# Gate and up of a feed-forward by Strassen's seven block products, in a kernel of two transformer blocks

## The chip, the cores and the metric

The kernel runs on one core of one Trainium2 chip. The metric is the device time of one execution in microseconds (us), the median of the runs shown.

## The reference, cut to what matters

Two blocks are computed one after the other on 512 tokens of 1024 channels (and 256 context tokens in the first), in float32. Among attention, a recurrent mixer and the modulation vectors they hold five feed-forwards; three of them (the latent tokens' in layer 1, and two in the second block) are what the change touches:

```python
def swiglu(h, w_in, w_out):              # h: 512 x 1024, hidden width 2816
    g, u = jnp.split(h @ w_in, 2, axis=-1)
    return (jax.nn.silu(g) * u) @ w_out
```

## The kernel before, in words

**Numbers.** Every product is made in three: both factors are split into a high part (rounded by ACT's copy to fp32r) and a low part (the rest), and high x high, low x high and high x low are added in PSUM (`product`, line 342). A weight block is [128, 8, 128] and comes by DMA into one of four `raw` slots (`load_block`, L308), ACT writes `w_hi` (`split_hi`, L317), POOL writes `w_lo` (`split_lo`, L323). The semaphores `hi_ready`, `lo_ready` and `w_used` count blocks over the whole program.

**A feed-forward** has 22 chunks of 128 hidden channels: a gate block, an up block and an out block for each. Group 0 to 9 (`ffn_groups`, line 1015, the `step` functions) takes four gate and up blocks (chunks 2g+1 and 2g+2) and two out blocks (chunks 2g and 2g+1); a last group, cut into token halves, follows. In a gate or up block PE does 8 x 3 products of 512 tokens (`in_block`, line 1029); for the out blocks 8 output tiles n, each 2 x 3 products, alternately in the PSUM banks 5 and 6. ACT takes the silu of the gate (L1197), DVE multiplies it with up (L1292), ACT and DVE split the hidden chunk (L1204, L1297), and DVE adds each output tile to `y` (L1357), which frees its bank. For l1_ffn and s_ffn1 DVE's queue also holds four modulation ops per group (`mods`, L406, and the copy of L460), 1024 columns each, fed by their own loads. s_ffn2 has none.

**What sets the order.** Each engine's queue is in program order, written out by hand in `ffn_pe`, `ffn_act`, `ffn_dve`, POOL's stage of `split_lo` and SP's stream of loads. The inner groups of the three feed-forwards are a hardware loop of two groups a turn; those of l0_ffn and l0_ffnc are unrolled. The feed-forwards l0_ffn and l0_ffnc are not touched.

## Time and profile before

| | |
|---|---|
| median of 3 runs | 2802.25 us (2801.66 to 2803.56) |
| profiled execution, span | 2801.8 us |
| PE busy | 2725.5 us (97%) |
| DVE, ACT, POOL busy | 1607.7, 1078.9, 1241.0 us |
| loaded weight blocks | 441 of 512 KB |

The profiled execution is one of its own, with 2801.8 us from its first to its last instruction; it is within the runs' spread. PE is TensorE, DVE VectorE, ACT ScalarE, POOL GpSimd, SP SyncE, which issues the loads. Busy PE time is modelled, since matmuls overlap; what one costs in a row of them is the distance between their starts. The granted clock is 1.00 at 2.4 GHz and 0.50 at 1.2 GHz.

### The profile page before, as it was taken

Reading aid. Unit: us, or ns where it says so; the run is one execution under the profiler, and the core shown is the slowest. Engines: PE = TensorE matmul, PEld = TensorE weight load, DVE = VectorE, ACT = ScalarE, POOL = GpSimd, SP = SyncE. Lnnn points to the kernel's source line nnn. Section 1 sums busy time; section 2 is a strip of 40 time slices with the busy share of each in tenths; the row PEclk is TensorE's granted clock in tenths of the full one; section 3 lists DMA queues with packets and bytes.
Section 4 is the critical chain, followed back from the end, with each engine's and each line's share of the span. In section 5 each row is a group of like instructions: output and inputs, shape, how many; then the busy total and the mean of one; then the engine's idle time right before and its main releaser. Section 6 shows DMA issues by size and latency. Waiting matters only on the chain.

```text
span 2801.8 us, 41300 instructions
## 1 busy us (share of the span) xinstructions
PE 2725.5 (97%) x15728; PEld 2353.3 (84%) x15728; DVE 1607.7 (57%) x2597; ACT 1078.9 (39%) x1817; POOL 1241.0 (44%) x646
## 2 busy tenths in 40 slices
PE   8989999999999999999999999999989999999998
PEld 6778888788999899988888888888877788888887
DVE  6788766677776678456556655555563512422223
ACT  3267332233445367442222332222464833422222
POOL 0333554445566433345544355444433344444443
PEclk8999999999999999999999999999999999999999
DMA  5323555443576422234544245442323233132221
GB/s 238 107 49 95 203 211 188 143 143 120 202 254 213 144 54 62 76 121 159 174 162 155 71 160 173 162 157 98 124 50 113 76 105 98 62 102 93 96 90 60
DMA packets 103865, 361.70 MB, mean 129 GB/s; under 512 B 12449, under 2 KB 14625, under 8 KB 102305
## 3 DMA queue, kind: packets, MB, share of 16 engines
q1 hardware_dynamic: 103714, 359.63, 38.6%
q8 instruction: 102, 1.67, 0.2%
q14 instruction: 49, 0.40, 0.0%
HBM read 338.61 MB, written 2.10 MB: 122 GB/s over the span
## 4 chain that ended last, share of the span: by engine, by line
PE 86%; DVE 8%; ACT 2%; issue 1%; POOL 1%; DMA 1%; POOLq 0%; SPq 0%; ACTq 0%; DVEq 0%
PE ps L346 73%; PE ps L2273 3%; PE ps L2261 2%; PE ps L2243 2%; PE ps L753 1%; DVE negm L2322 1%; PE ps L423 1%; PE ps L2466 1%; PE ps L573 1%; PE ps L2246 1%; PE ps L2028 1%; DVE dump L406 1%; POOL w_lo L323 1%; ACT prob L2295 0%; ACT w_hi L317 0%
## 5 line engine op out<-in xcount | busy, mean ns | idle before, releaser
L323 POOL TENSOR_TENSOR w_lo<-raw,w_hi 128x1024 fp32r<-128x1024 f32 x421 | 1076.4, 2565 | 1187.6 <-ACT w_hi L317 1156.2
L317 ACT ACTIVATE w_hi<-raw 128x1024 fp32r<-128x1024 f32 x441 | 460.4, 1056 | 1143.2 <-PE ps L346 1104.3
L346 PE MATMUL ps<-n_hi,w_hi 128*128 128x512 f32 (+1 forms) x1744 | 639.0, 366 | 10.5 <-DVE n_lo L880 9.5
L346 PE MATMUL ps<-n_lo,w_hi 128*128 128x512 f32 (+1 forms) x1744 | 627.2, 360 | 0.0
L346 PE MATMUL ps<-n_hi,w_lo 128*128 128x512 f32 (+1 forms) x1744 | 627.2, 360 | 0.0
L346 PEld LDWEIGHTS ps<-n_hi,w_hi 128*128 128x128 f32 x1744 | 328.6, 188 | 66.9 <-DVE n_lo L880 9.8
L346 PEld LDWEIGHTS ps<-n_lo,w_hi 128*128 128x128 f32 x1744 | 328.9, 189 | 51.0 <-issue 1.9
L346 PE MATMUL ps<-h_hi,w_hi 128*128 128x512 f32 (+1 forms) x1096 | 363.1, 346 | 8.8 <-DVE h_lo L622 4.4
L346 PEld LDWEIGHTS ps<-n_hi,w_lo 128*128 128x128 f32 x1744 | 328.6, 188 | 49.4
L346 PE MATMUL ps<-h_lo,w_hi 128*128 128x512 f32 (+1 forms) x1096 | 356.6, 340 | 0.0
L346 PE MATMUL ps<-h_hi,w_lo 128*128 128x512 f32 (+1 forms) x1096 | 356.5, 340 | 0.0
L346 PE MATMUL ps<-ffn_hi,w_hi 128*128 128x512 f32 (+1 forms) x928 | 334.0, 360 | 5.1 <-DVE y L1357 2.2
L346 PE MATMUL ps<-ffn_lo,w_hi 128*128 128x512 f32 (+1 forms) x928 | 332.9, 359 | 0.0
L346 PE MATMUL ps<-ffn_hi,w_lo 128*128 128x512 f32 (+1 forms) x928 | 332.6, 358 | 0.0
L1357 DVE TENSOR_TENSOR y<-y,ps 128x512 f32<-128x512 f32 x288 | 197.7, 687 | 188.5 <-PE ps L346 188.5
L1292 DVE TENSOR_TENSOR ps<-ffn_silu,ps 128x512 f32<-128x512 f32 (+1 forms) x107 | 68.3, 639 | 294.3 <-PE ps L346 272.1
L346 PEld LDWEIGHTS ps<-h_hi,w_hi 128*128 128x128 f32 x1096 | 201.6, 190 | 35.8 <-issue 10.3
L346 PEld LDWEIGHTS ps<-h_lo,w_hi 128*128 128x128 f32 x1096 | 201.1, 190 | 25.7 <-issue 2.2
L346 PEld LDWEIGHTS ps<-h_hi,w_lo 128*128 128x128 f32 x1096 | 200.8, 190 | 23.3
L346 PEld LDWEIGHTS ps<-ffn_hi,w_hi 128*128 128x128 f32 x928 | 175.6, 189 | 32.0 <-DVE y L1357 2.6
L406 DVE CUSTOM_DVE_ANT_0 dump<-mod_extra,modraw 128x1024 f32<-128x1024 f32 x93 | 197.8, 2127 | 4.3
L346 PEld LDWEIGHTS ps<-ffn_hi,w_lo 128*128 128x128 f32 x928 | 175.7, 189 | 25.8
(329 smaller groups left out, 3868.0 us busy)
## 6 DMA issues: line engine op xcount, KB each, us to landing
raw<-w_stream SPq DMA_DIRECT2D x441, 512.0 KB, 3.5
modraw<-mod_stream SPq DMA_DIRECT2D x88, 512.0 KB, 4.9
mod_extra<-mod_stream SPq DMA_DIRECT2D x88, 512.0 KB, 5.3
mod_pair<-mod_first SPq DMA_DIRECT2D x7, 1024.0 KB, 12.5
l_qs<-l_q_hi SPq DMA_DIRECT2D x32, 128.0 KB, 2.3
l_qs<-l_q_lo SPq DMA_DIRECT2D x32, 128.0 KB, 2.3
l_qs<-l_q_hi SPq DMA_DIRECT2D x16, 192.0 KB, 2.9
l_qs<-l_q_lo SPq DMA_DIRECT2D x16, 192.0 KB, 3.5
```

The source lines that it names most:

```text
L317: nc.scalar.activation(w_hi[:, c % RING, :], raw[:, c % RING, :], ACT.Copy).then_inc(hi_ready, 1)
L323: nc.gpsimd.tensor_tensor(w_lo[:, c % RING, :], raw[:, c % RING, :], w_hi[:, c % RING, :].bitcast(F32), ALU.subtract).then_inc(lo_ready, 1)
L346: mm = nc.tensor.matmul(out, w[a], x[b][:, off:off + n], start=first and i == 0, stop=last and i == 2)
L406: nc.vector.tensor_tensor_reduce(where, mod_slot(p), row, 1.0, 0.0, ALU.mult, ALU.add, outs[j]).then_inc(mod_ops, 1)
L423: mm = nc.tensor.matmul(ps[:, 3, 2 * k:2 * k + 2], mod_pairs[k][:, 0, j * P:(j + 1) * P], c_cols[:, j, :], start=j == 0, stop=j == KC - 1)
L573: mm = nc.tensor.matmul(ps[:, SUM_BANK[name] + i, 0:n], ones[:, :], buf, start=k == 0, stop=k == KC - 1)
L753: mm = nc.tensor.matmul(half(bank)[:, t * P + i:t * P + i + SUM_COLS], squares_[:, slot, t * P:(t + 1) * P], ones[:, 0:SUM_COLS], start=Tr ...
L1292: nc.vector.tensor_tensor(up_bank(f, m % 2), f["silu"][:, m % 2, 0:f["n"]], up_bank(f, m % 2), ALU.mult).then_inc(sem(f["tag"] + "_hid"), 1)
L1357: ins = nc.vector.tensor_tensor(acc, acc, out_bank(f, 8 * g + n), ALU.add)
L2243: mm = nc.tensor.matmul(score(a, i, col, w), a["qs"][head % 2][:, j, x[2]:x[2] + P], k[:, kc, kcol:kcol + w], start=j == 0, stop=j == 1 an ...
L2261: mm = nc.tensor.transpose(ps[:, 4 + g, (b - b0) * P:(b - b0 + 1) * P], prob[:, i % 2, b * P:(b + 1) * P], ident)
L2273: mm = nc.tensor.matmul(head_out(i), a["v"][z][:, blocks[b], a["vcol"](c, x)], a["pt"][p][:, i % 2, b * P:(b + 1) * P], start=b == 0 and j ...
```

## The change

In groups 1 to 9 of the three feed-forwards gate and up of a chunk are one product of a 2 x 2 block matrix (rows gate and up, columns the two halves of the 1024 channels) with a 2 x 2 block matrix of the input (channel halves by token halves), by the Winograd form of Strassen's scheme. With A11, A12 the gate's halves and A21, A22 the up's, the weight sides of the seven products are A11, A12, A22, S1 = A21 + A22, S2 = S1 - A11, S3 = A21 - A11 and S4 = A12 - S2. Each is four weight tiles by 256 tokens with three products each: 12 matmuls, 84 for a chunk in place of 48 of 512 tokens.

The input sides are four plain quarters' worth and four sums, made once per feed-forward in group 0: POOL adds high and low back into `full_in` (four ops of 1024 columns), DVE makes four sums of 1024, ACT their highs, DVE their lows. For each chunk POOL makes S1 and S3 (`down_pool`), ACT copies S1 to a PSUM bank, and DVE makes S2 and S4 there. The results are combined by DVE: ACT copies P1 = A11's product away (`seven_first_copy`), DVE adds it to S2's (`seven_u`), makes up's second half (`seven_c22`) and after the last product `F` (`seven_hidden`), then multiplies with the silu. The weights' highs and lows are now made in quarters of 512 columns, 18 items a group (seven for each chunk, four of the out blocks), in ten slots: two spare ones and the halves of the four old ones. The lows of S2 and S4 are DVE's, the others POOL's. The loops are unrolled, several semaphores become shared, three modulation slots remain of four, and the modulation ops of group 9 are split over two places.

```diff
+    full_in = at("full_in", [KC, S], HSPARE)
+    sum_hi = at("sum_hi", [4, 4, HC], HSPARE, F32R)
...
+    down_sum = at("down_sum", [2, 4 * P], SCR)
+    first_p, pair_u, pair_v = at("first_p", [HC], SCR + 4096), at("pair_u", [2, HC], SCR + 5120), at("pair_v", [HC], SCR + 7168)
...
-    TAIL_SLOTS = 4
+    TAIL_SLOTS = 3
...
-        if f["index"] == 0:
-            for g in range(NG - 1):
-                step(n0 + 6 * g, 0, (g, 0, 0))
+        for g in range(NG - 1):
+            step(n0 + 6 * g, 0, (g, 0, 0))
+        last(n0 + 6 * (NG - 1), NG - 1)
+    A11, S2, S3, S1, A12, A22, S4 = range(7)
+    PARTS, OUT_Q = 7, 14
+    ITEMS = 18
+    POOL_LOWS = [A11, S3, S1, A12, A22] + [PARTS + k for k in (A11, S3, S1, A12, A22)] + [OUT_Q, OUT_Q + 1, OUT_Q + 2]
+    DVE_LOWS = [S2, S4, PARTS + S2, PARTS + S4]
+    PE_ORDER = [A11, S2, S3, S1, A12, A22, S4] + [PARTS + k for k in (A11, S2, S3, S1, A12, A22, S4)]
+    SEVEN = NG - 2
+    Q_SLOTS = 10
...
+    def turn_of(g, k):
+        return ITEMS * (g - 1) + k + min(max(g - 2, 0), 4)
...
+    def slot_views(f, turn):
+        i = turn % Q_SLOTS
+        if i < 2:
+            return spare_q[i][0][:, :], spare_q[i][1][:, :]
+        slot, half_ = (f["c0"] + 4 + (i - 2) // 2) % RING, (i - 2) % 2
+        cols = slice(half_ * 4 * P, (half_ + 1) * 4 * P)
+        return w_hi[:, slot, cols], w_lo[:, slot, cols]
...
+    def slot_free(eng, f, turn):
+        old = turn - Q_SLOTS
+        if old >= 0 and item_at(old) is None:
+            old -= Q_SLOTS
+        if old >= 0:
+            item_used(eng, f, *item_at(old))
+        elif turn % Q_SLOTS >= 2:
+            eng.wait_ge(w_used, f["c0"] + 4 + (turn % Q_SLOTS - 2) // 2 + 1)
...
+    def item_hi(act, f, c, g, k):
+        item_ready(act, f, c, g, k)
+        turn = turn_of(g, k)
+        slot_free(act, f, turn)
+        ins = nc.scalar.activation(slot_views(f, turn)[0], item_raw(c, k), ACT.Copy)
+        if k == ITEMS - 1:
+            ins.then_inc(hi_ready, 6)
+        else:
+            ins.then_inc(q_hi, 1)
...
+    def raw_free(sp, f, c):
+        r = c - f["c0"] - 2
+        g, r = divmod(r, 6)
+        if not 1 <= g <= SEVEN:
+            sp.wait_ge(lo_ready, c + 1)
+        elif r == 5:
+            sp.wait_ge(lo_ready, c + 1)
+        else:
+            last = {0: A12, 1: A22, 2: PARTS + A12, 3: PARTS + A22, 4: OUT_Q + 2}[r]
+            low_there(sp, f, c - r, g, last)
+            if r in (0, 2):
+                sp.wait_ge(down_chain, 2 * chunks_done(f, g, r // 2) + 2)
...
+    def full_pool(pool, f, h, j):
+        if j == 0:
+            pool.wait_ge(h_half, chunks_before(h, 1) + KC)
+        ks = slice(2 * j, 2 * j + 2)
+        nc.gpsimd.tensor_tensor(full_in[:, ks, :], n_hi[:, ks, :].bitcast(F32), n_lo[:, ks, :].bitcast(F32), ALU.add).then_inc(in_full, 1)
+    def in_sums_dve(dve, f):
+        m = 8 * (f["index"] - 1)
+        def quarter(second, e):
+            return full_in[:, 4 * second:4 * second + 4, e * HC:(e + 1) * HC]
+        def out(i):
+            return sum_f[i // 2][:, i % 2, :, :]
+        dve.wait_ge(in_full, m // 2 + 2)
+        nc.vector.tensor_tensor(out(0), quarter(0, 1), quarter(0, 0), ALU.subtract).then_inc(in_sums, 1)
+        dve.wait_ge(in_full, m // 2 + 4)
+        nc.vector.tensor_tensor(out(2), quarter(0, 1), quarter(1, 1), ALU.subtract).then_inc(in_sums, 1)
+        dve.wait_ge(in_sums, m + 1)
+        nc.vector.tensor_tensor(out(1), quarter(1, 1), out(0), ALU.subtract).then_inc(in_sums, 1)
+        dve.wait_ge(in_sums, m + 3)
+        nc.vector.tensor_tensor(out(3), quarter(1, 0), out(1), ALU.subtract).then_inc(in_sums, 1)
...
+    def seven_pe(pe, f, c, g):
+        x = seven_inputs()
+        hid_ready, out_free, out_ready = sem(f["tag"] + "_hid_ready"), sem(f["out"] + "_out_free"), sem(f["out"] + "_out_ready")
+        place = {A11: (a_bank, 0), S2: (a_bank, 1), S3: (c_bank, 0), S1: (c_bank, 1), A12: (a_bank, 0), A22: (c_bank, 0), S4: (c_bank, 1)}
+        def one(b, k):
+            bank, e = place[k]
+            out = bank(b)[:, e * HC:(e + 1) * HC]
+            item = PARTS * b + k
+            low_there(pe, f, c, g, item)
+            hi, lo = slot_views(f, turn_of(g, item))
+            for kk in range(4):
+                cols = slice(kk * P, (kk + 1) * P)
+                for i, (w, z) in enumerate(((hi, 0), (hi, 1), (lo, 0))):
+                    mm = nc.tensor.matmul(out, w[:, cols], x[k][z][:, kk, :], start=k in (A11, S3) and kk == 0 and i == 0,
+                                          stop=kk == 3 and i == 2, skip_group_check=True)
+            mm.then_inc(q_used, 1)
+        def out_part(n, b):
+            hi, lo = slot_views(f, turn_of(g, OUT_Q + n // 4 * 2 + b))
+            cols = slice(n % 4 * P, (n % 4 + 1) * P)
+            return product((hi[:, cols], lo[:, cols]), (f["hi"][:, b, :], f["lo"][:, b, :]), [(out_bank(f, 8 * g + n), 0, S)], b == 0, b == 1)
+        def bank_free(n):
+            pe.wait_ge(out_free, f["free0"] + CREDIT + 8 * g + n + 1 - len(f["outs"]))
+        if g == 1:
+            pe.wait_ge(in_sums, 8 * f["index"])
+        pe.wait_ge(hid_ready, CREDIT + f["m"] + 2 * g)
+        for k in (A11, S2, S3, S1):
+            one(0, k)
+        pe.wait_ge(u_c22, 2 * chunks_done(f, g, 0) + 1)
+        one(0, A12)
+        pe.wait_ge(u_c22, 2 * chunks_done(f, g, 0) + 2)
+        one(0, A22)
+        one(0, S4)
+        pe.wait_ge(hid_ready, CREDIT + f["m"] + 2 * g + 1)
+        one(1, A11)
+        one(1, S2)
+        one(1, S3)
+        one(1, S1)
+        pe.wait_ge(u_c22, 2 * chunks_done(f, g, 1) + 1)
+        one(1, A12)
+        for b in range(2):
+            low_there(pe, f, c, g, OUT_Q + b)
+        for n in range(2):
+            bank_free(n)
+            out_part(n, 0)
+        pe.wait_ge(hid_ready, CREDIT + f["m"] + 2 * g + 2)
+        for n in range(2):
+            out_part(n, 1).then_inc(out_ready, 1)
+        for n in range(2, 4):
+            bank_free(n)
+            out_part(n, 0)
+            out_part(n, 1).then_inc(out_ready, 1)
+        pe.wait_ge(u_c22, 2 * chunks_done(f, g, 1) + 2)
+        one(1, A22)
+        one(1, S4)
+        for b in range(2):
+            low_there(pe, f, c, g, OUT_Q + 2 + b)
+        for n in range(4, KC):
+            bank_free(n)
+            out_part(n, 0)
+            mm = out_part(n, 1)
+            if n < KC - 1:
+                mm.then_inc(out_ready, 1)
+        mm.then_inc(w_used, 6)
...
+    def seven_first_copy(act, f, g, b):
+        i = chunks_done(f, g, b)
+        act.wait_ge(q_used, before_items(f, g, len(PE_ORDER)) + PE_ORDER.index(PARTS * b + S2) + 1)
+        if i >= 1:
+            act.wait_ge(u_c22, 2 * i - 1)
+        nc.scalar.activation(first_p[:], a_bank(b)[:, 0:HC], ACT.Copy).then_inc(act_copied, 1)
...
+    def seven_act(act, f, c, g):
+        def ahead(k):
+            if g < SEVEN:
+                item_hi(act, f, c + 6, g + 1, k)
+        for k in (PARTS + S2, PARTS + S3, PARTS + S1):
+            item_hi(act, f, c, g, k)
+        seven_first_copy(act, f, g, 0)
+        for k in (PARTS + A12, PARTS + A22, PARTS + S4):
+            item_hi(act, f, c, g, k)
+        seven_silu_first(act, f, g, 0)
+        item_hi(act, f, c, g, OUT_Q)
+        seven_silu_second(act, f, g, 0)
+        item_hi(act, f, c, g, OUT_Q + 1)
+        ffn_hidden_hi(act, f, 2 * g + 1, 0, c, 0)
+        seven_first_copy(act, f, g, 1)
+        item_hi(act, f, c, g, OUT_Q + 2)
+        item_hi(act, f, c, g, OUT_Q + 3)
+        if g < SEVEN:
+            ahead(A11)
+            down_copy(act, f, g + 1, 0)
+            for k in (S2, S3, S1):
+                ahead(k)
+        else:
+            prepare_last_act(act, f, c, 0)
+            prepare_last_act(act, f, c, 1)
+        seven_silu_first(act, f, g, 1)
+        if g < SEVEN:
+            down_copy(act, f, g + 1, 1)
+            ahead(A12)
+            ahead(A22)
+        else:
+            prepare_last_act(act, f, c, 2)
+        seven_silu_second(act, f, g, 1)
+        if g < SEVEN:
+            ahead(S4)
+            ahead(PARTS + A11)
+        ffn_hidden_hi(act, f, 2 * g + 2, 0, c + 6, 0)
+        if g == SEVEN:
+            prepare_last_act(act, f, c, 3)
...
+    def seven_s2(dve, f, c, g, b):
+        dve.wait_ge(act_copied, s1_copies(f, g, b))
+        raw_there(dve, c + 2 * b)
+        y = down_bank(b)
+        nc.vector.tensor_tensor(y, y, raw_quarter(c + 2 * b, A11), ALU.subtract).then_inc(down_chain, 1)
...
+    def seven_u(dve, f, g, b):
+        i = chunks_done(f, g, b)
+        dve.wait_ge(act_copied, p1_copies(f, g, b))
+        nc.vector.tensor_tensor(pair_u[:, b, :], a_bank(b)[:, HC:2 * HC], first_p[:], ALU.add).then_inc(u_c22, 1)
+    def seven_c22(dve, f, g, b):
+        i, m = chunks_done(f, g, b), 2 * g + 1 + b
+        dve.wait_ge(q_used, before_items(f, g, len(PE_ORDER)) + PE_ORDER.index(PARTS * b + S1) + 1)
+        dve.wait_ge(u_c22, 2 * i + 1)
+        link(dve, nc.vector.tensor_tensor(pair_v[:], c_bank(b)[:, 0:HC], pair_u[:, b, :], ALU.add))
+        nc.vector.tensor_tensor(f["silu"][:, m % 2, HC:2 * HC], c_bank(b)[:, HC:2 * HC], pair_v[:], ALU.add).then_inc(u_c22, 1)
+    def seven_hidden(dve, f, g, b):
+        m = 2 * g + 1 + b
+        dve.wait_ge(q_used, before_items(f, g, len(PE_ORDER)) + PE_ORDER.index(PARTS * b + S4) + 1)
+        u = pair_u[:, b:b + 1, :].to_broadcast([P, 2, HC])
+        both_ = c_bank(b).rearrange("p (e n) -> p e n", e=2)
+        nc.vector.tensor_tensor(both_, both_, u, ALU.add).then_inc(f_done, 1)
+        dve.wait_ge(sem(f["tag"] + "_silu"), f["m"] + m + 1)
+        dve.wait_ge(u_c22, 2 * chunks_done(f, g, b) + 2)
+        nc.vector.tensor_tensor(c_bank(b), c_bank(b), f["silu"][:, m % 2, :], ALU.mult).then_inc(sem(f["tag"] + "_hid"), 1)
...
+    def seven_dve(dve, f, c, g, mods):
+        out_ready, out_free = sem(f["out"] + "_out_ready"), sem(f["out"] + "_out_free")
+        def add(n):
+            if n < KC - 1:
+                dve.wait_ge(out_ready, f["ready0"] + (KC - 1) * g + n + 1)
+            else:
+                dve.wait_ge(w_used, c + 6)
+            acc = f["y"][:, n, :]
+            nc.vector.tensor_tensor(acc, acc, out_bank(f, 8 * g + n), ALU.add).then_inc(out_free, 1)
+        seven_u(dve, f, g, 0)
+        item_low_dve(dve, f, c, g, PARTS + S2)
+        seven_s4(dve, f, c, g, 1)
+        seven_c22(dve, f, g, 0)
+        item_low_dve(dve, f, c, g, PARTS + S4)
+        seven_hidden(dve, f, g, 0)
+        seven_u(dve, f, g, 1)
+        ffn_hidden_lo(dve, f, 2 * g + 1, 0)
+        mods(0)
+        seven_c22(dve, f, g, 1)
+        if g < SEVEN:
+            seven_s2(dve, f, c + 6, g + 1, 0)
+            item_low_dve(dve, f, c + 6, g + 1, S2)
+            seven_s4(dve, f, c + 6, g + 1, 0)
+        dve.wait_ge(out_free, f["free0"] + CREDIT + 8 * g)
+        for n in range(4):
+            add(n)
+        seven_hidden(dve, f, g, 1)
+        if g < SEVEN:
+            seven_s2(dve, f, c + 6, g + 1, 1)
+            item_low_dve(dve, f, c + 6, g + 1, S4)
+        for n in range(4, KC):
+            add(n)
+        ffn_hidden_lo(dve, f, 2 * g + 2, 0)
+        mods(1)
...
+    def down_pool(pool, f, c, g, b):
+        i = chunks_done(f, g, b)
+        raw_there(pool, c + 2 * b)
+        raw_there(pool, c + 2 * b + 1)
+        a11, a21, a22 = (raw_quarter(c + 2 * b, k) for k in (A11, S3, A22))
+        if i >= 2:
+            pool.wait_ge(act_copied, s1_copies(f, g, b) - 4)
+            pool.wait_ge(q_low_pool, len(POOL_LOWS) * ((i - 2) // 2) + POOL_LOWS.index(PARTS * b + S1) + 1)
+        nc.gpsimd.tensor_tensor(down_sum[:, b, :], a21, a22, ALU.add).then_inc(down_pair, 1)
+        pool.wait_ge(down_pair, 2 * i + 1)
+        nc.gpsimd.tensor_tensor(a21, a21, a11, ALU.subtract).then_inc(down_pair, 1)
+    def seven_pool(pool, f, c, g):
+        down_pool(pool, f, c, g, 0)
+        for k in (A11, S3, S1):
+            item_low_pool(pool, f, c, g, k)
+        down_pool(pool, f, c, g, 1)
+        for k in POOL_LOWS[3:]:
+            item_low_pool(pool, f, c, g, k)
+        item_low_pool(pool, f, c, g, ITEMS - 1)
...
+    def ffn_pool(pool, f, h):
+        c0 = f["c0"]
+        full_pool(pool, f, h, 0)
+        full_pool(pool, f, h, 1)
+        split_lo(pool, c0 + 4)
+        full_pool(pool, f, h, 2)
+        full_pool(pool, f, h, 3)
+        for i in range(5, 8):
+            split_lo(pool, c0 + i)
+        for g in range(1, SEVEN + 1):
+            seven_pool(pool, f, c0 + 2 + 6 * g, g)
+        for i in range(FFN_BLOCKS - RING, FFN_BLOCKS):
+            split_lo(pool, c0 + i)
...
+            if f["index"] > 0:
+                split_hi(act, c + RING)
+                ffn_silu(act, f, c, 0, 1)
+                split_hi(act, c + RING + 1)
+                ffn_hidden_hi(act, f, 1, 0, None, 0)
+                item_hi(act, f, c + 6, 1, A11)
+                in_sums_act(act, f)
+                down_copy(act, f, 1, 0)
+                for k in (S2, S3, S1):
+                    item_hi(act, f, c + 6, 1, k)
+                ffn_silu(act, f, c + 2, 0, 0)
+                down_copy(act, f, 1, 1)
+                for k in (A12, A22):
+                    item_hi(act, f, c + 6, 1, k)
+                ffn_hidden_hi(act, f, 2, 0, c + 6, 0)
+                for k in (S4, PARTS + A11):
+                    item_hi(act, f, c + 6, 1, k)
+                return
...
+            if f["index"] > 0:
+                in_sums_dve(dve, f)
             mods(g, 0, group)
+            if f["index"] > 0:
+                in_sums_low(dve, f)
+                seven_s2(dve, f, c + 6, 1, 0)
             ffn_mult(dve, f, 2 * g + 2, 2 * gd, c + 2, d)
+            if f["index"] > 0:
+                item_low_dve(dve, f, c + 6, 1, S2)
+                seven_s4(dve, f, c + 6, 1, 0)
             if f["held"]:
                 ffn_hidden_lo(dve, f, 2 * g + 2, 0)
...
+            if f["index"] > 0:
+                seven_s2(dve, f, c + 6, 1, 1)
+                item_low_dve(dve, f, c + 6, 1, S4)
```

## Rows read from the trace of the kernel before

**Rows 1.** The page: busy time by engine, and the chain that ended last.
```profile
PE 2725.5 (97%) x15728; PEld 2353.3 (84%) x15728; DVE 1607.7 (57%) x2597; ACT 1078.9 (39%) x1817; POOL 1241.0 (44%) x646
...
PE 86%; DVE 8%; ACT 2%; issue 1%; POOL 1%; DMA 1%; POOLq 0%; SPq 0%; ACTq 0%; DVEq 0%
```

**Rows 2.** By stretch: length, busy (count) PE, PEld, DVE, ACT, POOL; clock, DMA share, GB/s.
```profile
1257.00:1550.00 293.00, 293.00 (x1294) 242.60 (x1294) 174.27 (x202) 73.67 (x90) 147.18 (x54) 1.00 0.46 158
2460.00:2750.00 290.00, 290.00 (x1281) 240.15 (x1280) 72.76 (x106) 72.96 (x90) 126.72 (x53) 1.00 0.30 96
```

**Rows 3.** Timeline of PE (start, us, engine, line, op): out blocks, then the next group.
```profile
1311.23 0.39 PE L346 MATMUL ps<-ffn_hi,w_hi 128*128 128x512 f32 x1
...
1322.11 0.39 PE L346 MATMUL ps<-n_hi,w_hi 128*128 128x512 f32 x1
```

**Rows 4.** Timeline of PE, l0_ffnc: two 256-column products, 33 apart.
```profile
759.96 0.28 PE L346 MATMUL ps<-h_hi,w_hi 128*128 128x256 f32 x1
...
763.92 0.28 PE L346 MATMUL ps<-h_hi,w_hi 128*128 128x256 f32 x1
```

**Rows 5.** Groups by line, shapes apart: busy us, mean ns | idle before, releasers.
```profile
L1357 DVE TENSOR_TENSOR y<-y,ps 128x512 f32<-128x512 f32 x288 | 197.7, 687 | 188.5 <-PE ps L346 188.5
...
L1304 DVE TENSOR_TENSOR w_lo<-raw,w_hi 128x1024 fp32r<-128x1024 f32 x20 | 24.3, 1216 | 4.7 <-POOL w_lo L323 4.7
...
L1292 DVE TENSOR_TENSOR ps<-ffn_silu,ps 128x256 f32<-128x256 f32 x22 | 9.2, 420 | 5.7 <-ACT ffn_silu L1197 5.5
...
L317 ACT ACTIVATE w_hi<-raw 128x1024 fp32r<-128x1024 f32 x441 | 460.4, 1056 | 1143.2 <-PE ps L346 1104.3 <-DMA raw<-w_stream 26.7 <-PE ps L2466 11.9
L1204 ACT ACTIVATE ffn_hi<-ps 128x512 fp32r<-128x512 f32 x85 | 49.3, 580 | 13.1 <-DVE ps L1292 13.1
...
L1204 ACT ACTIVATE ffn_hi<-ps 128x256 fp32r<-128x256 f32 x22 | 8.3, 377 | 31.7 <-DVE ps L1292 30.9 <-PE ps L346 0.8
...
L2375 POOL TENSOR_SCALAR prob<-prob,rinv 128x512 f32<-128x512 f32 x40 | 27.9, 697 | 60.3 <-DVE rinv L2328 60.3
...
L2146 POOL TENSOR_TENSOR tsh<-tsh,loaded 128x512 f32<-128x512 f32 x9 | 11.6, 1290 | 37.8 <-DVE tsh L2088 37.8
```

**Rows 6.** Timelines of POOL, ACT and DVE in two groups of l1_ffn.
```profile
1301.69 2.40 POOL L323 TENSOR_TENSOR w_lo<-raw,w_hi 128x1024 fp32r<-128x1024 f32 x1 [1.79 <-ACT w_hi L317]
...
1322.31 2.01 ACT L317 ACTIVATE w_hi<-raw 128x1024 fp32r<-128x1024 f32 x2 [9.82 <-PE ps L346]
...
1323.45 9.09 POOL L323 TENSOR_TENSOR w_lo<-raw,w_hi 128x1024 fp32r<-128x1024 f32 x3 [8.48 <-ACT w_hi L317]
...
1324.83 0.69 DVE L1297 TENSOR_TENSOR ffn_lo<-ps,ffn_hi 128x512 fp32r<-128x512 f32 x1 [1.84 <-ACT ffn_hi L1204]
1325.44 1.49 DVE L406 CUSTOM_DVE_ANT_0 dump<-mod_extra,modraw 128x1024 f32<-128x1024 f32 x1
1326.98 3.30 DVE L406 CUSTOM_DVE_ANT_0 dump<-mod_extra,modraw 128x1024 f32<-128x1024 f32 x1
...
1330.42 2.13 DVE L460 COPY modv_l<-mod_acc 128x2 f32 x1
```

**Rows 7.** Timeline of DVE: the add of the first output tile, begun by PE at 1311.23.
```profile
1312.79 0.69 DVE L1357 TENSOR_TENSOR y<-y,ps 128x512 f32<-128x512 f32 x1 [0.57 <-PE ps L346]
```

**Rows 8.** Timeline of PE around three idle times; table by stretch for the clock.
```profile
553.52 0.50 PE L346 MATMUL ps<-ffn_hi,w_hi 128*128 128x512 f32 x1 [2.17 <-DVE y L1357]
...
557.97 0.39 PE L346 MATMUL ps<-ffn_hi,w_hi 128*128 128x512 f32 x1
...
1003.64 0.63 PE L2261 MATMUL ps<-loaded,prob 128*128 128x128 f32 x4 [1.80 <-DVE wide_pt_lo L2336]
...
1565.48 0.66 PE L753 MATMUL ps<-ones,post_squares 128*128 128x64 f32 x4 [1.42 <-POOL post_squares L737]
...
1005.00:1008.00 3.00, 2.35 (x13) 2.27 (x12) 2.51 (x7) 0.78 (x2) 2.79 (x3) 0.50 0.17 40
1565.50:1568.50 3.00, 3.00 (x26) 3.00 (x27) 0.69 (x1) 0.48 (x1) 1.30 (x2) 1.00 0.56 175
```

255 lines of the change are left out of this document (201 added, 54 removed).

## The prediction, on record before the changed kernel ran

> **What bounds the kernel now.** I read the busy times and the chain first [rows 1]: PE is busy for 97% of the span and holds 86% of the chain that ended last. The table by stretch [rows 2] says it for the stages of the change: from 1257 to 1550 us (l1_ffn) and from 2460 to 2750 (s_ffn2) PE has no idle time, at the full granted clock, while VectorE (DVE), ScalarE (ACT) and GpSimd (POOL) have slack. So here only PE's work counts, until another queue comes late. The timeline gives PE's pace: the 48 products of one group's out blocks fill 1311.23 to 1322.11, that is 0.2267 us per 512-column product [rows 3]; with 256 columns 33 products take 763.92 - 759.96, 0.120 us each, and PE still has no gap [rows 4]. A group of 144 products takes 32.64 us.
>
> **What the change saves.** A chunk's gate and up are now 48 x 0.2267 = 10.88 us; seven block products of 12 matmuls are 84 x 0.120 = 10.08. That is 0.80 us for each of 2 chunks x 9 groups x 3 feed-forwards = 54 chunks: **-43.2 us**; a group would take 31.04. The pace's bounds: 0.107 (half of the 0.213 us that 512 columns take at 2.4 GHz; then 102 us saved) and 0.1295, where nothing is saved; I keep 0.120, since it is measured with the same instruction and helper. The Trainium skill, page "TensorE: Matmul & The Clock Gate", section "Back-to-back issue gap", gives 262 cycles for 256 columns and 518 for 512; an estimate by it is 64 us saved in place of 43, and 21 us off my time. The rows here differ from it.
>
> **What it adds to the other queues.** Per op from [rows 5]: DVE 0.69 us for 512 columns with one operand in PSUM, 0.42 for 256, 1.22 for 1024 from SBUF; ACT 0.58 for 512 (the same as half of its 1.06 for 1024), 0.38 for 256; POOL 2.40 for 1024 and 1.29 for 512 (no w_lo of 512 is there; half of 2.40 and 1.29 bound it). In a row of ops the next starts 0.08 (DVE: 0.69 recorded, 0.61 to the next) or some 0.1 (ACT: two of 1.06 in 2.01) before the recorded end [rows 6], so I step 0.61 and 0.49. An add starts 0.20 us after PE's sixth product of its tile is through (1311.23 + 6 x 0.2267 = 1312.59, and 1312.79) [rows 3, 7]; other hand-overs I take at 0.06, a choice. I laid the queues beside each other in program order with these numbers; three waits of PE come out. Each is the chain of the others less what PE has to do meanwhile.
>
> Wait A, every group with a next one (8 per feed-forward): PE's out n=2 needs bank 5, freed by the first add of y. DVE reaches that add only behind S2, its low part and S4 of the *next* group's chunk, which need POOL's sum, which stands behind the last two lows of the out blocks, whose highs ACT makes only after it has copied P1 of the second chunk. From the end of that chunk's S2 product: 0.20 + P1 copy 0.25 + high 0.64; POOL 1.27 + 1.27 + sum 1.35; ACT copy 0.64; DVE S2 0.75; ACT high 0.64; DVE low 0.75, S4 0.61, add 0.75 = 9.12 us. PE meanwhile has S3, S1, A12 (36 x 0.120 = 4.32) and four out parts (12 x 0.2267 = 2.72), 7.04. It waits **2.09 us**.
>
> Wait B, out n=6: from the end of the second chunk's S4 product DVE must do F, ACT the silu, DVE mult, S2, low, add: 0.20 + 0.75 + 0.40 + 3 x 0.61 + 0.75 = 3.93 us against PE's 2.72: **1.21 us**. In groups 2 to 5 the slot numbering steps on by one, so the high of S1 waits until the second chunk's A22 product is done; then 0.20 + 0.64 + POOL 1.27 + 1.35 + ACT 3 x 0.49 + 0.40 + DVE 3 x 0.61 + 0.75 = 7.91 against 1.44 + 2.72: **3.76 us**.
>
> The start (group 0). POOL gets four 1024-column sums among its four lows, and DVE eight such ops from SBUF. POOL and DVE ops of this kind exclude each other: alone a modulation op takes about 1.22 us and a w_lo 2.40, but beside three w_lo the modulation ops took 1.49 and 3.30, the 2-column copy 2.13, and the three lows 9.09 for 3 x 2.40 [rows 6]; the adds from PSUM stay at 0.69 in the mean of all 288 [rows 5]. They take turns. Counted from PE's end of the first two blocks: POOL 8 x 2.39 + four turns of 1.2 = 23.9; its next three ops 3.8 and DVE's other four sums 4.7: 32.4; DVE S2 0.75, ACT three highs and silu 2.1, DVE mult, low, S4, add 2.7: 38.0 us. PE wanted out n=2 at 0.2 + 48 x 0.120 + 60 x 0.2267 = 19.6 (before, group 0 ends at 27.8). The rest of the outs, 8.2, and 1.7 of slow clock (below) end it at 47.8: **+20.0**. The Trainium skill, page "SBUF — State Buffer", section "SBUF: two separate sides", calls this pair of ports an exclusive lock for the whole instruction; by it the rival without turns (below) can't be, and the rows here agree.
>
> The modulation ops (l1_ffn and s_ffn1; s_ffn2 has none) stand in DVE's queue before u and c22, and POOL is now busy beside them. Two ops and the copy take 2 x 1.24 + 2 x 1.27 + some 0.2 = 5.2 us with POOL's turns. At the head of a group DVE comes to them 1.45 us in, so u ends at 7.1 where PE wants it after 5.76 (1.3 us), and c22 2.2 us later where PE wants it 1.44 later (0.7): **2.1 us** (3.2 in group 1). In the middle two turns of 1.24 and a new start of POOL's low make wait A **4.8 us** (3.15 in group 9).
>
> The clock. After an idle of 2.17 us before an out product PE ran at 1.2 GHz: 553.52 to 557.97 holds 12 products, 4.45 us for 2.72 [rows 8], 1.7 us lost; the clock fell to this level after 1.80 us too, and stayed at 2.4 GHz after 1.42. A's 2.09 us of lost issue is 1.93 of recorded idle. So I charge **1.7 us** after each A, each long B and each head wait of about 2 us in groups 1 and 3 to 6. Bounds: none, and one per wait.
>
> Sum, s_ffn2: 9 x -1.60 = -14.4; A 8 x 2.09 = 16.7; B 4 x 1.21 + 4 x 3.76 = 19.9; clock 12 x 1.7 = 20.4; start 20.0: +62.6 (a last 0.3 in group 9). With modulation, further: A 8 x 2.71 + 3.15 = 24.8; head waits 20; clock 6 x 1.7 = 10.2; start 2.6: +57.5, so +120 each. Together **+303 us**.
>
> Costed at nothing: the merged semaphores and the 3 modulation slots instead of 4 (those loads come as early as before; if DVE then waited for one, up to 5 us a load); the unrolled loop (l0_ffn is unrolled and runs at the same pace); SP's waits on quarters (the next chunk's blocks are asked for some 10 us before POOL reads them, landing takes 3.5 to 5, so if that cover went, A would grow by the rest); the last group's four highs.
>
> The profiled execution's span, 2801.8 us, stands 0.4 under the median of the runs, 2802.25. I predict 2802.25 + 303 = **3105 us**.
>
> **Rivals.** (1) Milder: the waits come, but the clock stays up (-80: 3024), or the ports don't take turns with 512-column ops (-142: 2963), or both (2896). For: wait A's 1.93 us is only 0.13 over the shortest idle with a fall; against: 1.49/3.30/2.13. (2) Faster: the queues reach the first add in time. It decides at one place: from the second chunk's S2 product to add n=0 in 7.04 us, not 9.12. POOL is the lever: at the 0.70 us that its 512-column scaling takes [rows 5] three ops save 1.8 and A is nearly gone. If the start is covered too but for blocks 4 and 5 (1.2 + 2.9 us late), the time is 2802 - 43 + 12 = 2771. Against it stands 1.29 for POOL's two-operand ops. (3) Between: A and B go, the start and head waits stay: 2805 to 2896. (4) The saving isn't there: if 256-column products here take 0.136 us and not 0.120, that adds 54 x 84 x 0.016 = 73: 3178.
>
> **Chances.** Forecast 0.60, its own range 3024 to 3165 (ops 5% longer add 31, hand-overs 10 to 13); rival 1 0.24; faster 0.07; rival 3 0.07; rival 4 0.01; no change 0.01. A measurement here tells 0.2% (5.6 us) from nothing. Range 2900 to 3165: rival 1 and the forecast; 2 in 10 stay out at most. So faster 0.07, same 0.01, slower 0.92.
>
> **What would show it.** Right: in the inner groups PE's 256-column products 0.120 us apart; PE idle before an out product, ended by DVE's add of y (about 1.9 to 4.6 us), twice a group; the granted clock at 0.5 for some 3.4 us after it; groups of about 36 us (40 in groups 2 to 5) in s_ffn2 and 41 to 47 with modulation; POOL and DVE ops of 1.2 to 3.3 us where they meet. Wrong: PE without gaps there (a group of 31 us), or idle that ends on a transfer or a low of POOL.

## The result, and the profile after

| | before | after |
|---|---|---|
| median, us (lowest to highest) | 2802.66 (2801.66 to 2803.56) | 3065.70 (3063.44 to 3068.23) |
| ratio, 95% interval | | 1.0938 [1.0922, 1.0953] |
| the profiled execution, us; its span | 2801.8 (span) | 3065.32; 3063.5 |

The change costs 263 us where 303 was forecast, inside the range. (The median before is of four executions here and of three in the table further up.) The page of the changed kernel, its busy times and the chain by engine; they answer to [rows 1]:

```profile
PE 2779.6 (91%) x17672; PEld 2459.5 (80%) x17672; DVE 1859.0 (61%) x3055; ACT 1254.3 (41%) x2315; POOL 1540.3 (50%) x982
...
PE 7%; DVE 2%; issue 2%; POOL 2%; ACT 1%; POOLq 0%; ACTq 0%; DVEq 0%
```

PE was busy for 97% of the span and is now for 91%; no other engine is near its limit. (The shares of the chain add up to 14% of the span only, so the waits have to be read elsewhere.) PE's waits in the changed kernel: who ended them, us in total, times, longest:

```profile
PE ps L356 <- DVE y L1452: 137.0, 51, 3.9
PE ps L356 <- DVE y L1875: 37.5, 3, 13.3
PE ps L1275 <- DVE pair_u L1422: 18.2, 18, 2.1
PE ps L356 <- POOL w_lo L333: 10.2, 8, 2.2
...
PE ps L1275 <- DVE ffn_silu L1429: 7.1, 17, 0.4
```

The first row is waits A and B (an out product waits for VectorE's add of y, line 1452), the second the starts (the copy to y of group 0), the third the heads of groups. By stretch (the columns of [rows 2]): group 0 of l1_ffn, its groups 1 to 10, and those of s_ffn2.

```profile
1223.00:1275.37 52.37, 36.38 (x181) 30.72 (x181) 34.81 (x37) 18.06 (x26) 35.83 (x17) 0.84 0.26 91
1275.37:1667.50 392.13, 326.57 (x2056) 292.35 (x2054) 243.35 (x356) 133.23 (x258) 239.00 (x159) 0.93 0.36 123
2692.28:3048.00 355.72, 322.01 (x2161) 294.59 (x2159) 160.24 (x269) 135.26 (x261) 205.72 (x160) 0.97 0.24 78
```

Where [rows 2] had PE without idle time at the full granted clock, it is idle 66 us of 392 in the second stretch and the mean granted clock is 0.93. PE's timeline shows the places (a wait stands in brackets):

```profile
1221.34 0.39 PE L356 MATMUL ps<-n_hi,w_hi 128*128 128x256 f32 x1 [0.74 <-DVE n_lo L890]
...
1241.91 0.80 PE L356 MATMUL ps<-n_hi,w_hi 128*128 128x512 f32 x1 [2.19 <-POOL w_lo L333]
...
1265.23 0.80 PE L356 MATMUL ps<-ffn_hi,w_hi 128*128 128x512 f32 x1 [13.30 <-DVE y L1875]
...
1283.39 0.38 PE L1275 MATMUL ps<-n_hi,w_hi 128*128 128x256 f32 x1 [2.11 <-DVE pair_u L1422]
...
1302.44 0.50 PE L356 MATMUL ps<-ffn_hi,w_hi 128*128 128x512 f32 x1 [3.85 <-DVE y L1452]
...
1306.88 0.28 PE L1275 MATMUL ps<-sum_hi,w_hi 128*128 128x256 f32 x1
...
1313.63 0.50 PE L356 MATMUL ps<-ffn_hi,w_hi 128*128 128x512 f32 x1 [0.96 <-DVE y L1452]
...
1356.92 0.50 PE L356 MATMUL ps<-ffn_hi,w_hi 128*128 128x512 f32 x1 [3.70 <-DVE y L1452]
...
1667.95 0.43 PE L763 MATMUL ps<-ones,post_squares 128*128 128x64 f32 x2 [1.41 <-POOL post_squares L747]
...
2714.31 0.50 PE L356 MATMUL ps<-ffn_hi,w_hi 128*128 128x512 f32 x1 [1.85 <-DVE y L1452]
...
2717.17 0.28 PE L1275 MATMUL ps<-sum_hi,w_hi 128*128 128x256 f32 x1
...
2744.05 0.40 PE L356 MATMUL ps<-ffn_hi,w_hi 128*128 128x512 f32 x1
```

From the first of these rows (the feed-forward's own first block) to the row at 1667.95 is l1_ffn's length, 446.6 us; the same two marks before stand at 1223.04 and 1565.48 [rows 8], 342.4 us. I use this length for every run below, counting at the end of each feed-forward its first sum of squares:

| length, us | before | after | lost |
|---|---|---|---|
| l1_ffn | 342.4 | 446.6 | +104.2 |
| s_ffn1 | 342.4 | 447.8 | +105.4 |
| s_ffn2 | 341.1 | 394.2 | +53.1 |

These three losses add up to 262.7 us, the whole change. VectorE (first eight rows), ScalarE and GpSimd ahead of the out product at 1302.44:

```profile
1292.91 2.00 DVE L416 CUSTOM_DVE_ANT_0 dump<-modraw 128x1024 f32<-128x1024 f32 x1
...
1295.07 2.08 DVE L416 CUSTOM_DVE_ANT_0 dump<-mod_extra,modraw 128x1024 f32<-128x1024 f32 x1
...
1297.19 1.13 DVE L470 COPY modv_l<-mod_acc 128x2 f32<-128x2 f32 x1
...
1298.68 0.42 DVE L1429 TENSOR_TENSOR ffn_silu<-ps,pair_v 128x256 f32<-128x256 f32 x1
1299.02 0.69 DVE L1412 TENSOR_TENSOR ps<-ps,raw 128x512 f32<-128x512 f32 x1
1300.37 0.69 DVE L1169 TENSOR_TENSOR w_lo<-ps,w_hi 128x512 fp32r<-128x512 f32 x1 [0.66 <-ACT w_hi L1143]
1301.10 0.70 DVE L1417 TENSOR_TENSOR ps<-raw,ps 128x512 f32<-128x512 f32 x1
1301.70 1.28 DVE L1452 TENSOR_TENSOR y<-y,ps 128x512 f32<-128x512 f32 x2
...
1298.33 0.60 ACT L1334 ACTIVATE ps<-down_sum 128x512 f32<-128x512 f32 x1 [4.83 <-POOL down_sum L1489]
...
1292.54 3.53 POOL L1159 TENSOR_TENSOR w_lo<-raw,w_hi 128x512 fp32r<-128x512 f32 x2 [0.86 <-ACT w_hi L1143]
1296.03 2.27 POOL L1489 TENSOR_TENSOR down_sum<-raw 128x512 f32<-128x512 f32 x1
```

This is the forecast's chain, op by op: GpSimd's lows and sum, ScalarE's copy, then S2, low, S4 and only then the add that frees the bank. GpSimd's sum takes 2.27 us here, and 1.29 at the same place once the modulation ops beside it are short (experiment 3); the modulation ops take 2.00 and 2.08 us.

### The profile page after: what moved, and what is told of

It is laid out like the page before. It is cut to its first block and busy times, and to the rows that moved or that the text cites. A ratio compares the mean times of both kernels' runs of the same rounds, so it can differ in the third digit from the quotient of the medians.

```text
span 3063.5 us, 45625 instructions
## 1 busy us (share of the span) xinstructions
PE 2779.6 (91%) x17672; PEld 2459.5 (80%) x17672; DVE 1859.0 (61%) x3055; ACT 1254.3 (41%) x2315; POOL 1540.3 (50%) x982
## 5 line engine op out<-in xcount | busy, mean ns | idle before, releaser
L333 POOL TENSOR_TENSOR w_lo<-raw,w_hi 128x1024 fp32r<-128x1024 f32 x259 | 658.5, 2548 | 686.5 <-ACT w_hi L327 622.7
L1159 POOL TENSOR_TENSOR w_lo<-raw,w_hi 128x512 fp32r<-128x512 f32 x261 | 360.8, 1390 | 279.8 <-ACT w_hi L1143 275.7
L327 ACT ACTIVATE w_hi<-raw 128x1024 fp32r<-128x1024 f32 x267 | 279.1, 1055 | 428.3 <-PE ps L356 391.6
L356 PE MATMUL ps<-n_hi,w_hi 128*128 128x256 f32 (+1 forms) x880 | 306.0, 348 | 18.5 <-DVE n_lo L890 9.5
L356 PE MATMUL ps<-n_hi,w_lo 128*128 128x256 f32 (+1 forms) x880 | 293.7, 334 | 0.0
L356 PE MATMUL ps<-n_lo,w_hi 128*128 128x256 f32 (+1 forms) x880 | 293.7, 334 | 0.0
L356 PEld LDWEIGHTS ps<-h_hi,w_hi 128*128 128x128 f32 x1096 | 201.7, 190 | 36.2 <-issue 10.6
L1143 ACT ACTIVATE w_hi<-raw 128x512 fp32r<-128x512 f32 x261 | 160.2, 626 | 120.3 <-PE ps L356 60.6
L2899 POOL TENSOR_SCALAR prob<-prob,rinv 128x768 f32<-128x768 f32 (+5 forms) x144 | 101.5, 705 | 211.0 <-DVE rinv L2852 211.0
L356 PEld LDWEIGHTS ps<-n_hi,w_hi 128*128 128x128 f32 x880 | 168.4, 191 | 43.0 <-DVE n_lo L890 9.8
L1275 PE MATMUL ps<-sum_hi,w_hi 128*128 128x256 f32 x684 | 195.5, 286 | 5.4 <-DVE ffn_silu L1429 5.4
```

Source lines behind the costliest of these rows:

```text
L327: nc.scalar.activation(w_hi[:, c % RING, :], raw[:, c % RING, :], ACT.Copy).then_inc(hi_ready, 1)
L333: nc.gpsimd.tensor_tensor(w_lo[:, c % RING, :], raw[:, c % RING, :], w_hi[:, c % RING, :].bitcast(F32), ALU.subtract).then_inc(lo_ready, 1)
L356: mm = nc.tensor.matmul(out, w[a], x[b][:, off:off + n], start=first and i == 0, stop=last and i == 2)
L1143: ins = nc.scalar.activation(slot_views(f, turn)[0], item_raw(c, k), ACT.Copy)
L1159: ins = nc.gpsimd.tensor_tensor(lo, item_raw(c, k), hi.bitcast(F32), ALU.subtract)
L1275: mm = nc.tensor.matmul(out, w[:, cols], x[k][z][:, kk, :], start=k in (A11, S3) and kk == 0 and i == 0, stop=kk == 3 and i == 2, skip_gro ...
```

## The experiments

Each kernel is the changed one with the edit shown. Where four executions were timed, the ratio to the kernel before, on the same chip, is given. The others were timed once; their effects on the total are 13 to 192 us, where executions of one kernel differ by 7 at most.

**1. VectorE's first adds ahead** (wait A):

```diff
+            dve.wait_ge(out_free, f["free0"] + CREDIT + 8 * g)
+            add(0)
             seven_s2(dve, f, c + 6, g + 1, 0)
+            add(1)
             item_low_dve(dve, f, c + 6, g + 1, S2)
             seven_s4(dve, f, c + 6, g + 1, 0)
-        for n in range(4):
+        for n in range(2, 4):
             add(n)
```

> Only VectorE's order inside a group is changed: the first add of y now stands ahead of S2 of the next group's chunk, the second ahead of its low part; everything is still computed. Theory (PE's wait before out n=2 is a place in VectorE's queue): in s_ffn2 out n=0 is through some 0.2 us after PE's ninth product, so the add ends 0.25 us after PE wants the bank; the wait falls from 1.85 to about 0 recorded, 2.0 to 0.25 of lost issue, 8 times: -14. With modulation c22 ends at 1299.02 and the add can end at 1299.7, PE restarts at 1299.9 and not at 1302.44: 8 x 2.5 x 2 = -40, and most of the clock falls behind these waits (16 x 1.7) go: -27. Together about -80, 2985 us (2970 to 3005). Rival (the same work only comes late elsewhere: GpSimd's lows or the second wait of the group take it up): waits before out n=6 grow from 0.96 and 3.70 by 1.5 us or more, total above 3045.

Measured: 2986.6 us; the lengths 412.3, 413.9 and 381.8, a gain of 34, 34 and 12. The waits on the add came from 137.0 to 87.0 us (PE's waits):

```profile
PE ps L356 <- DVE y L1452: 87.0, 51, 3.7
```

And PE's timeline, a wait A of l1_ffn and the first wait of s_ffn2's groups:

```profile
1302.62 0.50 PE L356 MATMUL ps<-ffn_hi,w_hi 128*128 128x512 f32 x1 [1.17 <-DVE y L1452]
...
2657.46 0.50 PE L356 MATMUL ps<-ffn_hi,w_hi 128*128 128x512 f32 x1 [1.45 <-DVE y L1452]
```

With modulation wait A is 1.17 instead of 3.85, and behind it the clock no longer falls; in s_ffn2 it is gone (0.17). The second row is wait B, short form, which grew from 0.96 to 1.45: the rival is right for half a microsecond, the order of VectorE's queue for the rest.

**2. Adds of out 4 and 5 and the silu ahead** (wait B):

```diff
         seven_hidden(dve, f, g, 1)
+        add(4)
+        add(5)
         if g < SEVEN:
             seven_s2(dve, f, c + 6, g + 1, 1)
             item_low_dve(dve, f, c + 6, g + 1, S4)
-        for n in range(4, KC):
+        for n in range(6, KC):
...
         if g < SEVEN:
+            seven_silu_second(act, f, g, 1)
             down_copy(act, f, g + 1, 1)
             ahead(A12)
             ahead(A22)
-        seven_silu_second(act, f, g, 1)
```

> Only the second wait of a group is touched: VectorE adds out n=4 and n=5 ahead of S2 and low S4 of the next group's second chunk, and ScalarE takes the second silu ahead of the copy of the down sum; everything is still computed. Theory (the wait before out n=6 is, in the short form, VectorE's two ops of the next chunk, and in groups 2 to 5 ScalarE's queue that stands behind GpSimd's sum): from the S4 product F 0.95, silu 0.35, product 0.65 and the add 0.65 end at 2.6 us, PE wants the bank at 2.72, so both forms go: 3 x (4 x 1.12 + 4 x 3.86) = -60, and the clock falls after the long form (12 x 1.7) -20: about 2985 (2975 to 3010). Rival (in groups 2 to 5 the slots themselves are late, so PE then waits for a low of GpSimd or VectorE at the next group's products): the 3.70 go, but waits of PE on w_lo or spare_lo of 1 to 3 us come in their place; total 3020 or more.

Measured: 2984.3 us; 27, 27 and 26 us gained. PE's waits (columns as above): of 51 on the add 27 are left, those of wait A.

```profile
PE ps L356 <- DVE y L1453: 81.2, 27, 3.9
...
PE ps L356 <- POOL w_lo L333: 10.2, 8, 2.2
```

No wait on a 512-column low part came in its place, so the rival is out. What held up the long form stands in the queues of the changed kernel, ahead of the out product at 1356.92: F (L1437) was begun at 1350.52, the silu (L1351) stood behind the copy (L1334), which waited for GpSimd's sum, and VectorE's product waited for the silu:

```profile
1350.52 0.70 DVE L1437 TENSOR_TENSOR ps<-ps,pair_u 128x512 f32<-128x512 f32 x1 [2.31 <-PE ps L1275]
...
1352.41 0.60 ACT L1334 ACTIVATE ps<-down_sum 128x512 f32<-128x512 f32 x1 [2.38 <-POOL down_sum L1489]
...
1353.99 0.36 ACT L1351 ACTIVATE ps<-ps 128x256 f32<-128x256 f32 x1
...
1354.38 0.70 DVE L1440 TENSOR_TENSOR ps<-ps,ffn_silu 128x512 f32<-128x512 f32 x1 [3.17 <-ACT ps L1351]
```

With the edit F is begun at 1349.03, the silu at 1349.76 and VectorE's product at 1350.16, and the copy comes behind them. So the numbering of the slots, which makes the sum late, costs nothing once silu and adds stand ahead of the next chunk's work. How much each of the two moves gave was not tried by itself.

**3. Modulation ops shortened**, in groups 1 to 9 of l1_ffn and s_ffn1:

```diff
+            if cols is not None:
+                where, wide, row = where[:, 0:cols], wide[:, 0:cols], row[:, 0:cols]
+            nc.vector.tensor_tensor_reduce(where, wide, row, 1.0, 0.0,
```

> Left out: the modulation ops of groups 1 to 9 of l1_ffn and s_ffn1 work on 64 of their 1024 columns; loads, waits and order stay. Theory (what these two feed-forwards lose beyond s_ffn2 is the modulation ops in VectorE's queue, and GpSimd's ops beside them): their groups become those of s_ffn2, wait before out n=2 from 3.85 to 1.85, head waits gone, GpSimd's 512-column ops near 1.3 us; the loss of a feed-forward from 104 to some 55: about -98, 2968 us (2960 to 2985). Rival (VectorE and GpSimd do not shut each other out, the ops only take their own 1.3 us): the waits shrink by less than their ops' time, and GpSimd's down sum in the groups stays at 2.27 us; total above 3000.

Measured: 2983.4 us; l1_ffn 405.4, s_ffn1 407.0, s_ffn2 394.5: 41 us less in each of the first two, nothing in the third. Wait A is 1.89 us there, close to s_ffn2's 1.85, and in PE's waits one head wait is left in each:

```profile
PE ps L356 <- DVE y L1455: 101.6, 51, 3.7
...
PE ps L1278 <- DVE pair_u L1425: 4.2, 2, 2.1
```

The theory holds for the place, and GpSimd's sum, 2.27 us at this place in the changed kernel, now takes its own time, so the rival is out:

```profile
1294.93 1.29 POOL L1492 TENSOR_TENSOR down_sum<-raw 128x512 f32<-128x512 f32 x1
```

15 us of the forecast gain are missing. In them are what the two starts with full ops lose beyond that of s_ffn2 (2.6 and 3.3 us), the heads left in group 1 (3.0 us or more each), and groups 3 to 6 of both, whose 144 products take 17.7 us where groups 2 and 7 to 9 take 17.27; the rest I didn't take apart.

**4. GpSimd's sum ahead of its last two lows**:

```diff
-        for k in POOL_LOWS[3:]:
+        for k in POOL_LOWS[3:-1]:
             item_low_pool(pool, f, c, g, k)
+        if g < SEVEN:
+            down_pool(pool, f, c + 6, g + 1, 0)
+        item_low_pool(pool, f, c, g, POOL_LOWS[-1])
         item_low_pool(pool, f, c, g, ITEMS - 1)
```

> Only GpSimd's order: the down sum and difference of the next group's first chunk stand ahead of the last two lows of the out blocks; everything is still computed. Theory (the chain of wait A runs P1 copy, highs, GpSimd's lows, its sum, ScalarE's copy, VectorE's S2, low, S4, add): in s_ffn2 the sum comes 2.5 us earlier, and the wait of 1.85 goes to about 0.2: -14 and some 5 of clock. With modulation it gains nothing, because there S2 starts at 1299.02 when VectorE is through with c22 behind the modulation ops, with the sum's copy only just done: the wait stays near 3.85. Total about 3047 (3040 to 3055). Rival (the sum alone sets the wait everywhere): all waits before out n=2 lose 2 us or more and their falls go, total 2985 to 3010. Rival (last lows now late): waits before out n=4 on w_lo.

Measured: 3018.4 us, outside the theory's range and the rival's; 16, 15 and 18 us gained. No wait on w_lo before out n=4 came. In s_ffn2 wait A is gone, as expected. With modulation it fell to 3.07 where I expected 3.85, and these rows of VectorE and GpSimd say why:

```profile
1295.04 1.21 DVE L416 CUSTOM_DVE_ANT_0 dump<-modraw 128x1024 f32<-128x1024 f32 x1
...
1296.40 2.08 DVE L416 CUSTOM_DVE_ANT_0 dump<-mod_extra,modraw 128x1024 f32<-128x1024 f32 x1
...
1300.36 0.69 DVE L1412 TENSOR_TENSOR ps<-ps,raw 128x512 f32<-128x512 f32 x1
...
1293.76 1.30 POOL L1489 TENSOR_TENSOR down_sum<-raw 128x512 f32<-128x512 f32 x1
1295.14 2.27 POOL L1491 TENSOR_TENSOR raw<-raw 128x512 f32<-128x512 f32 x1
```

S2 does start when VectorE is through with c22, as I said, with the sum long made; but the first modulation op now takes 1.21 us and not 2.00, since it had the turn and GpSimd's next op waited instead. I had moved a queue and, in the forecast, left the turns where they were. (8 x 0.78 us of waits are 6 of the 16 gained there. Most of the rest is the clock, which fell after four of these eight waits and before after all eight; see the last section.)

**5. The start**: ScalarE's silu ahead of the highs of the sums; on VectorE

```diff
-                in_sums_dve(dve, f)
-            mods(g, 0, group)
-                in_sums_low(dve, f)
-                seven_s2(dve, f, c + 6, 1, 0)
-            ffn_mult(dve, f, 2 * g + 2, 2 * gd, c + 2, d)
+                in_sums_dve(dve, f, (0,))
+                mods(g, 0, group)
+                in_sums_dve(dve, f, (2, 1, 3))
+                ffn_mult(dve, f, 2 * g + 2, 2 * gd, c + 2, d)
+                copy_out(0)
+                for i in range(4):
+                    copy_out(1 + i)
+                    in_sums_low(dve, f, (i,))
```

> Only group 0 of the three feed-forwards: VectorE's modulation ops stand after its first input sum, its eight copies to y between the four low parts of the sums (and the next chunk's ops between the last copies), ScalarE's silu ahead of the highs of the sums; everything is still computed. Theory (the 13.3 us before out n=2 are VectorE's queue; PE could go on as soon as the sums end at 1249.5): of the +20.2 us of the start in l1_ffn about 9 stay (VectorE's sums end 2.3 us later, GpSimd's w_lo keep PE 2.2 us), in s_ffn2 6 of 17.6: -11, -11 and -12, 3031 us (3022 to 3042). Rival (the start is bound by GpSimd and VectorE in sum, their work is only moved): the wait goes from out n=2 to the first products of group 1 on VectorE's sums or lows, and less than 5 us a feed-forward are gained, total above 3050.

Measured: 3052.5 us, only 13 gained (3.4, 6.7 and 4.8 us by length). The start itself did fall from +20.2 to +8.6 us, as the theory said, but group 1 of l1_ffn grew from 41.1 to 49.4 us. In PE's waits two others have grown in place of the one of 13.3 us, that on u from 18.2 us and a longest of 2.1, that on w_lo from 10.2 and 2.2:

```profile
PE ps L1274 <- DVE pair_u L1421: 34.2, 19, 8.1
PE ps L356 <- POOL w_lo L333: 12.1, 8, 3.2
```

The rival held in the main (s_ffn1 gained more than its 5 us): the work is moved, not hidden. Two further kernels leave some of it out, which prices it. The first:

```diff
-            return sum_hi[:, i, :, :], sum_lo[i // 2][:, i % 2, :, :]
+            return plain(0, 0)
...
-            return sum_f[i // 2][:, i % 2, :, :]
+            return sum_f[i // 2][:, i % 2, :, 0:16]
```

> The changed kernel, and left out: the sums of the inputs (GpSimd's full_in on 32 of its 512 columns a tile, VectorE's sums and low parts and ScalarE's highs on 16 of 256, and the products that would read them read a plain quarter); all else stays. Theory (the start's +20.2, +20 and +17.6 are these ops and what they hold up): the wait of 13.3 us before out n=2 and the 2.2 us on w_lo go: -51, 3015 us (3005 to 3030). Rival (the start is late through S2 and S4 of the next chunk and the modulation ops in VectorE's queue): half or more of the 13.3 stays, total above 3040.

Measured: 3023.7 us; 13.6, 13.6 and 14.2 us gained. That is the least that the input sums cost, because their ops are short here but still take turns (VectorE's second to fourth sum, of 64 columns, took 2.43, 1.33 and 1.33 us beside GpSimd's ops). In l1_ffn a wait of 4.15 us on the copy stays, with S2, S4 and the modulation ops in front of it in VectorE's queue, and the rest of the +20.2 with it. Both theories had a part. The second:

```diff
-        nc.gpsimd.tensor_tensor(full_in[:, ks, :], n_hi[:, ks, :].bitcast(F32), n_lo[:, ks, :].bitcast(F32), ALU.add)
+        nc.gpsimd.tensor_tensor(full_in[:, ks, 0:32], n_hi[:, ks, 0:32].bitcast(F32), n_lo[:, ks, 0:32].bitcast(F32), ALU.add)
```

> The changed kernel, and left out: only GpSimd's four sums full_in (32 of 512 columns a tile); VectorE's sums keep their size and read the high part of the input. Theory (GpSimd's part works twice: its own 10.5 us, and turns with VectorE that make its sums 3.34 us and not 1.2): GpSimd's low parts are in time, VectorE's four sums take 1.2 to 2.4 us each, and the wait before out n=2 falls from 13.3 to about 7: -8.5 for each feed-forward, 3040 us (3030 to 3050). Rival (VectorE's own eight ops and the two modulation ops are enough to make the wait): above 10 us of it stays, total above 3055.

Measured: 3049.0 us; 6.5, 6.9 and 3.3 us. The total is in the theory's range, the wait is the rival's: 11.96 us of it stay where the theory had 7. GpSimd only goes on to its next ops and VectorE still takes turns with them. VectorE and GpSimd in this kernel:

```profile
1237.55 3.42 DVE L1235 TENSOR_TENSOR sum_f<-n_hi 128x1024 f32<-128x1024 f32 x1
1240.89 2.31 DVE L1237 TENSOR_TENSOR sum_f<-n_hi,sum_f 128x1024 f32<-128x1024 f32 x1
...
1231.76 8.12 POOL L333 TENSOR_TENSOR w_lo<-raw,w_hi 128x1024 fp32r<-128x1024 f32 x3
1239.84 2.27 POOL L1489 TENSOR_TENSOR down_sum<-raw 128x512 f32<-128x512 f32 x1
```

**6. Together**: 1, 2 and 5.

> The three changes of order together (the first adds ahead; the adds of out n=4 and 5 ahead, the silu ahead; the start). Everything is still computed. Theory (three separate waits of PE, each an order in a queue): the gains add, -79, -81 and that of the start alone (-34 by my estimate): 2871 us (2860 to 2890). Rival (the queues are full, so a wait removed comes back elsewhere): less than three quarters of the sum is gained, above 2915, with waits of PE on GpSimd's lows.

Measured: 2873.9 us, as the theory said. Alone they gained 79, 81 and 13, together 192: 18 more than the sum, of which the growth of wait B to 1.45 in experiment 1, which can't come here, is one part; the rest I didn't take apart. In s_ffn2 a group now takes 31.66 us (two equal places of neighbouring groups, 2577.48 and 2609.14) where the products of before take 32.64 (by [rows 3]) and those of the change alone 31.04.

**7. To a version that pays?** Next, 6 with 4, the modulation ops one by one into VectorE's gaps, and c22 of the second chunk behind the first add:

```diff
         item_low_dve(dve, f, c, g, PARTS + S4)
+        mods(0, 0)
         seven_hidden(dve, f, g, 0)
...
-        mods(0)
-        seven_c22(dve, f, g, 1)
+        mods(0, 1)
+        mods(1, 0)
...
             add(0)
+            seven_c22(dve, f, g, 1)
...
         for n in range(2, 4):
             add(n)
+        mods(1, 1)
```

> The three changes of order, GpSimd's sum ahead of the last two lows, and the modulation ops spread: one after the low part of S4 of the second chunk, two after the low part of the first hidden chunk, the fourth after the add of out n=3; c22 of the second chunk after the first add. Everything is still computed. Theory (with the waits on order gone, a group costs its products, 31.04 us, and about 0.4 for c22 of the first chunk; only the start is left): against the kernel before 27 x -1.2 = -32 and the starts +9, +9, +6: 2795 us (2785 to 2815), so the saving of the products and the cost of the start about cancel. Rival (VectorE with the modulation ops and GpSimd shutting each other out fill a group of 31 us: 26 us of VectorE's and 26 of GpSimd's own work): groups with modulation stay at 33 us or more, total 2825 or more.

Measured: 2851.2 us, ratio 1.0172 [1.0155, 1.0189]: a total of the rival's (2825 or more), 56 us over mine. Groups 2 to 5 with modulation take 32.24 us and 6 to 8 take 32.97, just under the rival's 33, but 0.8 to 1.5 over my 31.44; s_ffn2's take 32.24 too. That is some 20 of the 56. The larger part comes right behind the starts, which end where I had them (+8.6, +8.5 and +6.7 us): PE waits 8.0 us for u in group 1, which takes 43.6 us (38.0 in s_ffn2). Then ScalarE's copies of group 0:

```diff
+                    nc.scalar.activation(f["y"][:, n, :], out_bank(f, n), ACT.Copy).then_inc(sem(f["out"] + "_out_free"), 1)
```

> As the run before, and in group 0 of the three feed-forwards ScalarE makes the eight copies to y in place of VectorE, between the highs of the sums. Everything is still computed. Theory (the start is VectorE's work; 8 x 0.61 us of it go to ScalarE, idle there): the start loses 3 to 5 us less per feed-forward, 2783 us (2775 to 2800), below the kernel before by 0.3 to 0.9%. Rival (GpSimd's eight double turns set the start): nothing is gained over the run before, within 4 us.

Measured: 2845.0 us, ratio 1.0147 [1.0131, 1.0164]; the copies are worth 1.6 to 2.6 us a feed-forward, less than my 3 to 5 and more than the rival's nothing. (The forecast of 2783 was on record with the 2795 of the run before, and carries its miss.) Lengths 360.3, 361.1 and 347.3. The next kernel fits the orders to each feed-forward:

```diff
-                in_sums_dve(dve, f, (0,))
-                mods(g, 0, group)
-                in_sums_dve(dve, f, (2, 1, 3))
+                in_sums_dve(dve, f, (0, 2, 1, 3))
...
                 seven_s4(dve, f, c + 6, 1, 0)
+                mods(g, 0, group)
...
-                mods(g, 1, group)
...
+        if g == 1:
+            before_mods()
         mods(0, 0)
```

> As the run with ScalarE's copies, and: where there is modulation the order is first add, c22, second add, then S2 of the next group; in s_ffn2, where there is none, c22 stands ahead of the adds again (its groups took 31.66 us so, and 32.24 with c22 behind). In group 0 the modulation ops stand behind S4 of the next chunk, where VectorE was idle for 5.6 us, and the second pair in group 1. Everything is still computed. Theory: the groups come to 31.7 (9 x -0.5 in each feed-forward, -14 together), and in the two starts with modulation the sums end 5 us earlier and the 5.73 before u go, -8 each: 2815 us (2805 to 2830), still above the kernel before, since the starts are worth more than the 4 us that nine groups of 31.7 save beyond 32.64. Rival (GpSimd and VectorE together fill the start, so the order there is worth nothing): only the groups' part is gained, 2831 or more.

Measured: 2855.4 us, ratio 1.0183 [1.0166, 1.0200], above the run before, with two opposite parts. s_ffn2 took 341.6 us, 0.5 above its 341.1 of before, with groups of 31.63 us. The two with modulation took 369, 9 and 8 us more than in the run before. In l1_ffn the start ended 2.1 us earlier; group 1 took 46.1 us (40.6 before), and groups 2 to 8 took 33.1 to 33.8 where they had taken 32.24 to 33.1 and I had forecast 31.7, since the wait before out n=6, 0.6 us at most before, was now 1.2 to 1.7. So the new order inside the groups is wrong too, by some 5 us. What the postponed modulation ops did to group 1 is in SyncE's waits from 1230 to 1300 us (columns as PE's):

```profile
SPq L404 <- DVE mod_acc L416: 27.2, 4, 19.1
```

and in GpSimd's timeline:

```profile
1271.20 1.26 POOL L1514 TENSOR_TENSOR down_sum<-raw 128x512 f32<-128x512 f32 x1 [6.27 <-DMA raw<-w_stream]
```

SyncE stood 27.2 us before loads of modulation tiles (2.7 in the run before), and the weight blocks stood behind them in its queue, so that GpSimd waited 6.27 us for one. The prediction had put SyncE's waits at nothing, since the blocks are asked for some 10 us before GpSimd reads them; here they came too late. PE waited 9.1 us for u (5.7 in the run before). Last, the best order of each feed-forward, and in two of them on GpSimd

```diff
+        if f["index"] > 1:
+            split_lo(pool, c0 + 5)
         full_pool(pool, f, h, 2)
         full_pool(pool, f, h, 3)
```

> As the run with ScalarE's copies, with two parts changed by feed-forward. In s_ffn2 c22 stands ahead of the adds again. In s_ffn1 and s_ffn2 GpSimd's low part of the fourth block of group 0 stands ahead of its last two input sums, and ScalarE copies two outputs before it waits for the sums; l1_ffn stays as in that run. Everything is still computed. Theory (VectorE's and GpSimd's orders in single places set what is left; each place can be read in one feed-forward): l1_ffn stays at 360.3 us, s_ffn1 loses 2 us less (359; PE's wait of 3.2 us on w_lo goes, the sums come 2.4 us later), s_ffn2 comes from 347.3 to 339 (341.6 with the other run's order of c22, less 2 to 3), the first of the three below its 341.1 of before; total 2834 us (2828 to 2842), still above the kernel before. Rival (the start is GpSimd's and VectorE's sum of work, so an earlier low part only makes the input sums late): s_ffn1 at 361 or more, s_ffn2 at 341.5 or more, total 2838 to 2842.

Measured: 2843.2 us, ratio 1.0141 [1.0124, 1.0158], a microsecond above both ranges; lengths 360.8, 362.2 and 344.6. The rival held for the start: GpSimd's earlier low part only moved PE's wait to its next one (4.46 us before the outs in s_ffn1) and made PE wait 9.1 and 5.3 us for u (5.7 and 1.8 in the run with ScalarE's copies). No version ran faster than the kernel before; the nearest is 1.4% above it.

## Why the forecast was right, point by point

| term, us, l1_ffn / s_ffn2 | forecast | measured |
|---|---|---|
| products | -14.4 / -14.4 | -14.4 / -14.4 |
| start | +22.6 / +20.0 | +20.2 / +17.6 |
| wait A | +41.6 / +16.7 | +34.5 / +16.1 |
| wait B | +19.9 / +19.9 | +19.9 / +19.9 |
| heads of groups | +20 / 0 | +17.5 / 0 |
| clock behind the waits | +30.6 / +20.4 | +23.2 / +10.6 |
| sum / length's change | +120 / +62.6 | +100.9, +104.2 / +49.8, +53.1 |

The signs that the prediction named came: PE idle before an out product until VectorE's add of y, twice a group, and groups of 34.5 to 36.1 us in s_ffn2 (38.6 to 40.4 in groups 2 to 5) and of 40.2 to 44.9 with modulation.

- **Products.** 144 of them fill 17.27 us (2726.78 to 2744.05), 0.120 each: the row measured with the same instruction was the right price, and with it the saving of 0.80 us a chunk. In experiment 6 a group of s_ffn2, 31.66 us against 32.64, shows it with most waits gone.
- **Wait A** was right in s_ffn2 (lost issue 2.24 - 0.23 = 2.01 forecast 2.09). With modulation it lost 4.01 where I took 4.8: I let GpSimd stand for two whole ops of 1.24 us and start anew; its two lows took 3.53 us for 2.55 and its sum 2.27 for 1.28, together 1.97 more. (The modulation ops with their copy took 5.34 us, forecast 5.2.) Experiments 1 and 4 show the cause.
- **Wait B**: 1.35 - 0.23 = 1.12 (forecast 1.21) and 4.09 - 0.23 = 3.86 (forecast 3.76), in exactly the groups named. Experiment 2 shows the cause.
- **Heads**: group 1 lost 3.03 us (forecast 3.2), groups 3 to 6 2.13 (2.1), the other four 1.46 (2.1).
- **Start**: 2.4 us too dear in both. VectorE and GpSimd in turns are seen in its rows, and leaving out the input sums gave back 14 us of it; the parts do not come off one by one (experiment 5).
- **Clock**: the step that was mis-sized. "I charge 1.7 us after each A": where the clock fell it cost 1.4 to 2.7 us, mostly 1.6, but in s_ffn2 it fell after 3 of 8 waits A only, and after no head wait (the longest, 2.11 us, included). That is 9.8 us, a little more than the 9.5 by which s_ffn2 came out below its forecast, and 7.4 of l1_ffn's 15.8; wait A with modulation is 7.1 of it. Of rival 1 the half about the clock was thus right, in part: neither always nor never.
- The table's sum misses the lengths by 3.3 us. I had not charged that PE needs some 0.14 us more for the twelve products behind a wait (2714.31 to 2717.17, 2.86 for 2.72), which is 2.2 us for the 16 waits A and B; the rest stays open. These 3.3 us hide as much of the other terms, all of which came out at or below their forecast.
- The rivals without turns, without A and B, and without the saving are all excluded by rows above. SyncE's queue and the three modulation slots show no cost in the changed kernel (VectorE waits 4.6 us in all for modulation tiles, 4.0 before), until an experiment postponed what frees them.

## What to carry to other kernels

Fewer products pay only if the engines that prepare them stay ahead: here 43 us of PE's time were bought with 299 us more of GpSimd's busy time and 251 us more of VectorE's (their turns included), and PE gave 306 back in waits and slow clock. Look first at where the add that frees a bank stands in its queue, and put it ahead of whatever prepares the next group: two reorderings of a few lines, each tried alone, gave back 79 and 81 of the 263 us. And when work that releases a load is postponed, look at what else stands in the load queue behind it.

## What the runs showed of the hardware

- The granted clock's fall behind a wait of PE is not a matter of the wait's length alone between 1.8 and 3.1 us. The twelve products behind a wait of 1.85 us in s_ffn2 took 2.86 us (full clock) five times and 4.29 to 4.46 three times, under the same work; behind 3.07 us in experiment 4 they took 2.85 (from 1303.78) and 4.46 (from 1383.19). Behind waits of 3.69 to 3.86 us in the changed kernel they always took 4.27 to 5.29, behind 1.16 to 1.18 us in experiment 1 always 2.85 to 2.90. The forecast's rule, a fall from 1.80 us on, came from two rows. What decides between these I did not find.
- VectorE's copy of 2 columns takes 0.17 us by itself and 1.10 to 1.14 beside GpSimd's 512-column ops; of a pair of ops that meet, the later one pays (in experiment 4 the modulation op at 1295.04 takes 1.21 us and GpSimd's op at 1295.14 takes 2.27). The Trainium skill, page "SBUF — State Buffer", section "SBUF: two separate sides", calls the pair of ports an exclusive lock held for the whole instruction; the 2.27 us of GpSimd's 1.28 us ops and experiment 4, where the same op took 1.21 us for 2.00 after a change of order on the other engine, agree.
- The turns are seen only where all operands of VectorE's op stand in SBUF: its ops with an operand in PSUM keep their time beside GpSimd (0.42 us for 256 columns at 1298.68, 0.69 for 512 at 1299.02 in the changed kernel), and so does GpSimd's (1.27 us at 1298.37). Shortening four of GpSimd's ops (experiment 5, last kernel) gave 17 us in all, though they had taken 10.5 us in each of three starts: GpSimd's next ops met VectorE's sums instead.
